# Output tiles that take the products with the high part of the activations first, and wait for them chunk by chunk

## The reference

```
h    = rmsnorm(x, norm1_g) * (1 + sc1) + sh1
q_a, k_a, v_a, beta, alpha, z_a, q_b, k_b, v_b, u_c, gates = split(h @ w_in)
o_a  = gated_deltanet(...);  o_b = differential_attention(...);  o_c = hyena(...)
merged = sum over j of sigmoid(gates_j) * (o_j @ w_br_j)
x    = x + g1 * (merged @ w_out)
hf   = rmsnorm(x, norm2_g) * (1 + sc2) + sh2
gate, up = split(hf @ w_ffn_in)
x    = x + g2 * ((silu(gate) * up) @ w_ffn_out)
```

## Time and profile before

| | us |
|---|---|
| median of 3 runs (lowest to highest) | 3982.35 (3978.43 to 3986.39) |
| the profiled execution | 3979.51 |
| its span, first to last instruction | 3977.7 |
| TensorE matmuls busy | 3424.3 (86%) |
| GpSimd busy | 1437.6 (36%) |
| VectorE busy | 1432.8 (36%) |
| ScalarE busy | 817.8 (21%) |

### The profile page before, as it was taken

The page is one execution under the profiler, slowest core; times in us unless marked ns, Lnnn a source line. Parts: engine busy times, 40 slices in busy tenths (PEclk is TensorE's granted clock), DMA queues, the critical chain, the costliest instruction groups (busy, mean ns, idle before and its releaser), DMA issues.

```text
span 3977.7 us, 55062 instructions
## 1 busy us (share of the span) xinstructions
PE 3424.3 (86%) x21792; PEld 3061.2 (77%) x21792; DVE 1432.8 (36%) x2231; ACT 817.8 (21%) x1639; POOL 1437.6 (36%) x1088
## 2 busy tenths in 40 slices
PE   6978887877889987999987888797688998799997
PEld 5967777546569987999977777684384898799996
DVE  2067773355432122111122667705553222211112
ACT  3133332232110112010022333313311111200001
POOL 0454442002215543444424444320040354344443
PEclk8989998877799998999988999997797999899999
DMA  4201112111112211222211111121120121122221
GB/s 163 75 33 43 43 43 75 56 43 51 49 39 75 75 64 53 70 76 70 77 60 58 43 43 45 52 67 44 44 77 28 53 75 64 53 75 69 70 75 69
DMA packets 62882, 242.62 MB, mean 61 GB/s; under 512 B 6961, under 2 KB 6961, under 8 KB 61489
## 3 DMA queue, kind: packets, MB, share of 16 engines
q1 hardware_dynamic: 60336, 224.77, 17.6%
q10 hardware_dynamic: 1728, 12.36, 0.8%
q0 software_dynamic: 576, 2.10, 0.2%
HBM read 234.48 MB, written 4.72 MB: 60 GB/s over the span
## 4 chain that ended last, share of the span: by engine, by line
PE 66%; issue 10%; DVE 9%; POOLq 5%; POOL 4%; ACT 2%; DVEq 2%; DMA 1%; ACTq 0%; SPq 0%
PE ps_G L582 27%; PE ps_GPM L582 26%; POOLq L2002 5%; PE ps_M L960 2%; POOL gu_hi L1985 1%; DVE small L1735 1%; PE ps_GPM L613 1%; PE ps_G L848 1%; POOL gu_lo L1985 1%; POOL big L2011 1%; PE ps_M L905 1%; PE ps_M L662 1%; DVE big L1766 1%; PE ps_M L988 1%; PE ps_M L887 1%
## 5 line engine op out<-in xcount | busy, mean ns | idle before, releaser
L1949 POOL CAST w_hi<-ring 128x1024 fp32r<-128x1024 f32 x296 | 310.1, 1048 | 1596.7 <-PE ps_G L582 983.8
L1951 POOL TENSOR_TENSOR w_lo<-ring,w_hi 128x1024 fp32r<-128x1024 f32 x296 | 740.9, 2503 | 51.8 <-issue 8.9
L582 PE MATMUL ps_G<-room_a,w_hi 128*128 128x320 f32 x1984 | 455.7, 319 | 92.6 <-DVEq L1434 61.9
L582 PE MATMUL ps_GPM<-room_a,w_hi 128*128 128x320 f32 x1984 | 437.5, 309 | 0.0
L582 PEld LDWEIGHTS ps_G<-room_a,w_hi 128*128 128x128 f32 x1984 | 346.4, 196 | 95.8 <-DVEq L1434 63.7
L582 PE MATMUL ps_G<-room_b,w_hi 128*128 128x320 f32 x1408 | 369.0, 315 | 24.0 <-DVEq L1434 24.0
L582 PE MATMUL ps_G<-room_o,w_hi 128*128 128x320 f32 x1280 | 337.4, 313 | 44.3 <-DVEq L1434 44.3
L582 PE MATMUL ps_GPM<-room_b,w_hi 128*128 128x320 f32 x1408 | 361.4, 309 | 0.0
L582 PE MATMUL ps_GPM<-room_o,w_hi 128*128 128x320 f32 x1280 | 332.9, 309 | 0.0
L582 PEld LDWEIGHTS ps_GPM<-room_a,w_hi 128*128 128x128 f32 x1984 | 331.9, 188 | 0.0
L2001 POOL TENSOR_TENSOR outs<-big,con 128x512 f32<-128x512 f32 x168 | 208.7, 1242 | 296.7 <-DVEq L1582 190.5
(11 more groups left out here) (392 smaller groups left out, 5941.4 us busy)
## 6 DMA issues: line engine op xcount, KB each, us to landing
ring<-in_W SPq DMA_DIRECT2D x416, 512.0 KB, 3.5
big<-in_INV ACTq DMA_DIRECT2D x2, 1664.0 KB, 6.8
par<-in_PARAMS ACTq DMA_DIRECT2D x2, 1646.0 KB, 8.9
big<-in_FWD ACTq DMA_DIRECT2D x2, 1632.0 KB, 8.0
x<-in_X SPq DMA_DIRECT2D x1, 2560.0 KB, 8.9
out_Y<-h SPq DMA_DIRECT2D x1, 2560.0 KB, 7.5
con<-in_CONSTS SPq DMA_DIRECT2D x1, 1364.0 KB, 11.7
sc<-in_HYCS ACTq DMA_DIRECT2D x2, 578.5 KB, 3.5
```

What stands on the lines that cost most here:

```text
L582: m = pe.matmul(ap, w[wi][:, k, n0:n0 + P], acts[ai][k][:, a:b], start=(k == 0 and i == 0), stop=(k == chunks - 1 and i == 2))
L1949: nc.gpsimd.tensor_copy(hi, raw)
L1951: nc.gpsimd.tensor_tensor(wlo[:, slot * UNIT:(slot + 1) * UNIT], raw, hi.bitcast(F32), ALU.subtract)
```

## The change

- `by_parts` goes. `tile_product` now runs in two passes over the chunks: first, for each chunk, weights-high and weights-low with the high activation; then, for each chunk, weights-high with the low activation. Inside a chunk each weight tile is used for the half in the first bank, then for the half in the second. The 48 products and their weight loads are the same.
- The first tile of a stage gets `ready`: a semaphore and a value for the high part and for the low part. Before each chunk of either pass TensorE waits for that chunk's tile. The single waits ahead of the stages go.
- `low_tiles` and the low tiles of the mix branches signal at each tile, not behind the drain; the drain stays, without a signal.
- `shift` writes each piece twice: rounded into the stage's high tiles, then shifted in place into `h`; the last of the four instructions of a chunk signals its high tile. The `round_tiles` behind norm1 (stage A) and behind norm2 (f1) go, and VectorE's wait for `h_ready` there.

```diff
-            def by_parts(ap, w, n0, acts, a, b, chunks=KC, turned=None):
-                for k in range(chunks):
-                    for i, (wi, ai) in enumerate(((0, 0), (0, 1), (1, 0))):
-                        m = pe.matmul(ap, w[wi][:, k, n0:n0 + P], acts[ai][k][:, a:b], start=(k == 0 and i == 0),
-                                      stop=(k == chunks - 1 and i == 2))
...
-                by_parts(tile[:, 0:HALF], w, n0, acts, 0, HALF, chunks, fl_a)
-                return by_parts(tile[:, HALF:NT], w, n0, acts, HALF, NT, chunks, fl_b)
+                for weights, part in (((0, 1), 0), ((0,), 1)):
+                    for k in range(chunks):
+                        if ready is not None:
+                            done, value, per = ready[part]
+                            pe.wait_ge(done, value + k // per)
+                        for wi in weights:
+                            for a, b, fl in ((0, HALF, fl_a), (HALF, NT, fl_b)):
+                                first = k == 0 and wi == 0 and part == 0
+                                m = pe.matmul(tile[:, a:b], w[wi][:, k, n0:n0 + P], acts[part][k][:, a:b], start=first,
+                                              stop=(k == chunks - 1 and part == 1))
+                                if first:
+                                    m.then_inc(fl, 1)
+                return m
...
-                pe.wait_ge(h_split.sem, h_split.at(L, 2))
                 for i in range(0, 2):
-                    products("B", "t", 0, L, i, h_b)
+                    products("B", "t", 0, L, i, h_b, ready=None if i else h_tiles(L, 1))
...
-                    pe.wait_ge(act_ready, L * (FT // 2) + ((first + n) // 2))
+                    pairs = L * (FT // 2) + first // 2 + 1
                     for i in range(0, 2):
-                        products(f"f2_{g}", "t", 0, L, i, act_f, n)
+                        products(f"f2_{g}", "t", 0, L, i, act_f, n, None if i else ((act_hi, pairs, 2), (act_ready, pairs, 2)))
...
-            def shift(layer, k0, mod_at):
+            def shift(layer, k0, mod_at, acts, sem_):
                 for k in range(KC):
                     act.wait_ge(hnorm.sem, hnorm.at(layer, k0 + k + 1))
-                    nc.scalar.activation(hv[:, k, 0:NS], hv[:, k, 0:NS], ACT.Identity,
-                                         bias=modv[:, mod_at + k, 0:1])
-                    nc.scalar.activation(hv[:, k, NS:NT], hv[:, k, NS:NT], ACT.Identity,
-                                         bias=modv[:, mod_at + k, 1:2])
+                    for q, (a, b) in enumerate(((0, NS), (NS, NT))):
+                        bias = modv[:, mod_at + k, q:q + 1]
+                        nc.scalar.activation(acts[0][k][:, a:b], hv[:, k, a:b], ACT.Identity, bias=bias)
+                        m = nc.scalar.activation(hv[:, k, a:b], hv[:, k, a:b], ACT.Identity, bias=bias)
+                    m.then_inc(sem_, 1)
                 act.drain()
...
-                shift(L, 0, 0)
+                shift(L, 0, 0, h_a, hi_ready.sem)
                 act.drain().then_inc(h_ready.sem, 1)
-                round_tiles(htiles, h_a, hi_ready.sem)
...
-                    tt(acts[1][k], src[k], acts[0][k].bitcast(F32), ALU.subtract)
-                dve.drain().then_inc(done, 1)
+                    tt(acts[1][k], src[k], acts[0][k].bitcast(F32), ALU.subtract).then_inc(done, 1)
+                dve.drain()
...
                 scale(0, L, rms_ready.at(L, 1))
-                dve.wait_ge(h_ready.sem, h_ready.at(L, 1))
                 low_tiles(htiles, h_a, hi_ready.sem, hi_ready.at(L, 1), h_split.sem)
```

More of the change, by code:

```diff
@@ L408, in trunk_program @@
         unit_split = sem("unit_split")
[L409 to L412, removed]
+        h_split = sig_("h_low_tiles_ready", 4 * KC)
+        o_split = sem("o_low_tiles_ready")
+        m_split = sig_("merged_low_tiles_ready", KC)
+        hf_split = sig_("h_ffn_low_tiles_ready", KC)
         inverse_done = sem("inverse_done")
@@ L575, in parts, with tile_product @@
                         wlo[:, lo * UNIT:(lo + 1) * UNIT].rearrange("p (k n) -> p k n", n=n))
-            def by_parts(ap, w, n0, acts, a, b, chunks=KC, turned=None):
-                for k in range(chunks):
-                    for i, (wi, ai) in enumerate(((0, 0), (0, 1), (1, 0))):
-                        m = pe.matmul(ap, w[wi][:, k, n0:n0 + P], acts[ai][k][:, a:b], start=(k == 0 and i == 0),
-                                      stop=(k == chunks - 1 and i == 2))
[L584 to L588, removed]
+            def tile_product(phase, name, t, layer, step, w, n0, acts, chunks=KC, ready=None):
                 _, fl_b = fill(phase, name + "_b", layer, step)
@@ L601, in fill, with products, h_tiles @@
                 return ap, fl
-            def products(phase, prefix, k, layer, step, acts, chunks=KC):
+            def products(phase, prefix, k, layer, step, acts, chunks=KC, ready=None):
                 for t in range(4):
                     w = parts(phase, k + t, layer, step)
-                    tile_product(phase, f"{prefix}{t}", t, layer, step, w, 0, acts, chunks).then_inc(unit_used, 1)
+                    tile_product(phase, f"{prefix}{t}", t, layer, step, w, 0, acts, chunks, None if t else ready
+                                 ).then_inc(unit_used, 1)
+            def h_tiles(layer, n):
+                return (hi_ready.sem, hi_ready.at(layer, n * KC + 1), 1), (h_split.sem, h_split.at(layer, n * KC + 1), 1)
             def modulation(k, slot, number):
@@ L664, in _ @@
                 m.then_inc(fl, 1)
-                pe.wait_ge(h_split.sem, h_split.at(L, 1))
                 for i in range(0, 4):
-                    products("A", "t", 0, L, i, h_a)
+                    products("A", "t", 0, L, i, h_a, ready=None if i else h_tiles(L, 0))
                 pe.wait_ge(g_ready.sem, g_ready.at(L, 1))
@@ L922, in _ @@
                     pe.matmul(ap[:, 0:P], ones, osq[:, NS:NT], start=True, stop=True).then_inc(fl, 1)
-                pe.wait_ge(h_split.sem, h_split.at(L, 3))
                 for i in range(0, 3):
-                    products("C", "t", 0, L, i, h_c)
+                    products("C", "t", 0, L, i, h_c, ready=None if i else h_tiles(L, 2))
                 pe.wait_ge(hyc_in.sem, hyc_in.at(L, 16))
@@ L997, in _ @@
                 m.then_inc(fl, 1)
-                pe.wait_ge(h_split.sem, h_split.at(L, 4))
                 for b in range(0, 3):
                     for half in range(2):
-                        products("mix", f"g{half}_", 6 * half, L, b, h_b)
-                        if half == 0:
-                            pe.wait_ge(o_split, L * 3 + b + 1)
+                        products("mix", f"g{half}_", 6 * half, L, b, h_b, ready=h_tiles(L, 3) if b + half == 0 else None)
+                        o_at = (L * 3 + b) * 4 + 1
                         for s in range(2):
@@ L1009, in _ @@
                             for t in range(2):
-                                m = tile_product("mix", f"b{half}_{2 * s + t}", t, L, b, w, t * P, o_m, 4)
+                                m = tile_product("mix", f"b{half}_{2 * s + t}", t, L, b, w, t * P, o_m, 4,
+                                                 ((om_hi, o_at, 1), (o_split, o_at, 1)) if half + s + t == 0 else None)
                                 if t == 0:
@@ L1013, in _ @@
                             m.then_inc(unit_used, 1)
-                pe.wait_ge(m_split.sem, m_split.at(L, 1))
                 for i in range(0, 2):
-                    products("out", "t", 0, L, i, h_b)
+                    products("out", "t", 0, L, i, h_b, ready=None if i else (
+                        (mg_hi.sem, mg_hi.at(L, 1), 1), (m_split.sem, m_split.at(L, 1), 1)))
                 sum_squares("norm2", L, hv, KC, sq_ready)
-                pe.wait_ge(hf_split.sem, hf_split.at(L, 1))
                 for g, (first, n) in enumerate(F_GROUPS):
                     for i in range(0, n // 2):
-                        products(f"f1_{g}", "t", 0, L, i, h_f)
-                    pe.wait_ge(act_ready, L * (FT // 2) + ((first + n) // 2))
+                        products(f"f1_{g}", "t", 0, L, i, h_f, ready=None if g + i else (
+                            (hf_hi.sem, hf_hi.at(L, 1), 1), (hf_split.sem, hf_split.at(L, 1), 1)))
+                    pairs = L * (FT // 2) + first // 2 + 1
                     for i in range(0, 2):
-                        products(f"f2_{g}", "t", 0, L, i, act_f, n)
+                        products(f"f2_{g}", "t", 0, L, i, act_f, n, None if i else ((act_hi, pairs, 2), (act_ready, pairs, 2)))
             sum_squares("norm1", DEPTH, hv, KC, sq_ready)
@@ L1394, in _ @@
                 rms_root("norm2", L)
-                shift(L, KC, 24)
+                shift(L, KC, 24, h_f, hf_hi.sem)
                 act.drain().then_inc(h_ready.sem, 1)
-                round_tiles(htiles, h_f, hf_hi.sem)
                 for g, (first, n) in enumerate(F_GROUPS):
@@ L1872, in _ @@
```

(4 more changed lines are left out.)

1 line of the change is left out of this document (removed).

## The result

The changed kernel takes 3892.9 us (median of 4 runs, 3892.3 to 3893.8), the kernel before beside it 3984.0 (3978.4 to 3986.4): a ratio of 0.977 [0.976, 0.979], some 91 us by the medians. The forecast was 3897, with 3882 to 3926 as range, and a sum of -85.6 us.

A forecast was written before the change was run, and what follows sets the result against it. TensorE's output-tile products, idle 130.2 and 30.6 us waiting for VectorE's queue, were taken as the bound. Terms of -42.8 us a layer, -85.6 for two, from the median 3982.35 give 3896.8 (forecast 3897); range 3882 to 3926.

The forecast's parts named there:

- A: Stage A behind norm1: the double shift writes take 1.86 us a chunk, a loss of 5.8 us per layer.
- f1: First tile of f1: ends at 1515.9 where it ended at 1520.42, -4.5 us per layer, ends -6.9 and -1.3.
- mix and out: Starts of mix and out: the first product moves earlier, -6.0 and -7.1 us per layer, each within 1.5 us.
- C: First tile of C: ends 0.4 us after the last low tile, -9.6 us per layer; low end 7.2.
- f2: Starts of the three f2 groups: waits shrink or go, -6.8, -7.6 and -6.3 us, together -20.7 us per layer.
- The clock stays low while chunks trickle in: Rival, chance 0.18: first tiles of C, mix, out and f1 run wholly at 1.2 GHz, 30 us back, 3926.
- The costly order: Rival, chance 0.06: gaps at each bank change lower the clock; with a tenth of the tiles +168 us, 4065.
- The faster pitch: Rival, chance 0.04: the new order makes all 14016 products faster, 188 us less, 3709.

The follow-up runs named there:

- the kernel with the rounds: The changed kernel with the norms of before (shift in place, then eight rounds), chunk waits kept: 3877.3 us, ratio 0.9742 against the kernel before.

## Why the prediction was right, step by step

The mechanism held: single waits for VectorE went, one for one, with the low clock behind them, and the norms' part lost in A. That the sum came within 0.4 us in the first layer is partly luck: mix and out together fell short by 2.2 us, and f1, C with the stages before it, and A made up 2.1 of it. One reading was short and entered no sum: by 0.267 us a product, first tiles of 8.67 to 10.08 us ran 3.6 to 6.8 us at the lower clock, not 3 to 6.

**f2** came out within 0.2 us in every group: 6.84, 7.62 and 6.14 us against 6.8, 7.6 and 6.3. The third group waits once for its last low pair (0.17 us, where 0.4 was worked out; then the 0.04 "issue" and the four products from 1919.18 in the chain above).

**C** was right in size and in what ends it. From ScalarE's first round the next tile starts at 11.4 us (935.95 to 947.35) where it was 20.96 (931.29 to 952.25): -9.56. The last low tile ends at 946.75 and the tile 0.6 us later. The table by stretch has the granted clock up again during the high products, so the low ones follow VectorE at full speed and the next tile does not start slow; the low end of this term's bounds was not needed:

```profile
936.80:943.00 6.20, 6.17 (x31) 6.20 (x32) 5.94 (x6) 4.28 (x7) 0.00 (x0) 0.71 0.28 75
943.00:947.30 4.30, 3.69 (x20) 2.65 (x19) 3.91 (x9) 0.00 (x0) 0.00 (x0) 1.00 0.15 62
```

Stages V and attention, whose code is as before, make the rest of that row of the table, 0.4 us in the first layer.

**mix and out** were mis-sized by 1.4 and 0.8 us, inside the 1.5 given for them. The start moved as forecast: from ScalarE's first round to the first product it is 0.88 us in place of 6.82 at mix, and 0.89 in place of 7.98 at out, -5.9 and -7.1. The term that failed is the tile itself, which I left as long as before: 9.85 in place of 8.67, and 9.67 in place of 8.91. Its surplus over 7.04, divided by the 0.12 us between 0.267 and 0.147, gives 23 and 22 products at the lower clock, where it was 14 and 16. In these rows from mix the clock stands at 0.50 (1.2 GHz) over the first 4.8 us although TensorE has almost no gap (4.74 us busy), and has risen in the stretch behind:

```profile
1146.20:1151.00 4.80, 4.74 (x18) 4.77 (x19) 4.80 (x7) 4.80 (x8) 0.00 (x0) 0.50 0.00 0
1151.00:1156.10 5.10, 5.10 (x34) 5.10 (x33) 3.91 (x3) 2.02 (x4) 0.00 (x0) 0.90 0.00 0
```

The extra products show that it is the clock. Why it takes longer than in the kernel before stays open: with the same code around it, mix's first tile took 9.86 us in one layer and 8.81 in the other of the kernel with the rounds. Over the traces without extra products it took 8.66 to 9.29 us in the eight first tiles with the single wait, and 8.55 to 9.86 us in the eight with chunk waits. The means, 9.0 and 9.5 us, lie 0.5 us apart, so much of the 1.2 us may be scatter.

**A** lost 6.1 us from the first shift to the projection's start (9.07 to 15.16) against 5.8. The chunk takes 1.81 us, not 1.86:

```profile
66.48 0.72 ACT L1096 ACTIVATE room_b<-h,modc 128x512 fp32r<-128x512 f32 x1 [5.38 <-DVEq L1493]
67.11 0.71 ACT L1097 ACTIVATE h<-h,modc 128x512 f32<-128x512 f32 x1
67.72 0.39 ACT L1096 ACTIVATE room_b<-h,modc 128x128 fp32r<-128x128 f32 x1
68.01 0.39 ACT L1097 ACTIVATE h<-h,modc 128x128 f32<-128x128 f32 x1
68.30 0.71 ACT L1096 ACTIVATE room_b<-h,modc 128x512 fp32r<-128x512 f32 x1
...
80.67 0.38 ACT L1097 ACTIVATE h<-h,modc 128x128 f32<-128x128 f32 x1
81.64 2.53 PE L667 MATMUL ps_M<-par,h 128*128 128x16 f32 x11 [21.31 <-ACTq L1106]
```

The short piece overlaps its neighbour as assumed (0.29 us apart, 0.39 long). So the chunks take 0.3 us less than forecast; between the end of the last shift and the projection lie 0.6 us, which were 0.1 before. (The table has 5.6, since this norm began 0.6 us earlier in the profiled execution.) In the second layer the loss from VectorE's first scaling to the projection is 5.6 us, but the scaling itself comes 1.3 us earlier after f2: in the kernel before, the chain goes there over the transfer of the layer's parameters (9.37 us), in the changed kernel over the sums of squares. That the second layer repeats the first was right within 0.2 us but for A and the stretch up to C. The kernel with the norms' part alone and the one without it show the loss from both sides, +9.5 and -12 us.

**f1** gained 1.5 us more than the term. The last high tile comes at 14.6 us (1479.81 to 1494.40), not 15.0. The 20 products behind it took 4.22 us, not 5.3: the clock came up while they ran, the case that I had put at the end of the bounds. In the stretches before, it had not:

```profile
1481.80:1489.00 7.20, 5.71 (x16) 4.14 (x16) 6.49 (x13) 7.20 (x17) 0.00 (x0) 0.50 0.00 0
1489.00:1494.80 5.80, 4.66 (x13) 3.46 (x14) 4.50 (x7) 5.39 (x12) 0.00 (x0) 0.50 0.00 0
1494.80:1498.70 3.90, 3.90 (x22) 3.90 (x22) 0.45 (x1) 0.00 (x0) 0.00 (x0) 0.75 0.00 0
```

What the prediction did not see is that this term has nothing to do with the direct writes: the chunk waits alone, on the old rounds, bring the same 18.8 us.

**The rivals.** "The clock stays low while chunks trickle in" holds at f1, where 29 products ran at 0.50 over 13 us, but not as a rule: in the kernel with one write in norm2 it rose to 1.00 while f1's chunks still trickled in. In C, mix and out the clock rose, and no first tile ran wholly at the low one; of its 30 us for two layers, mix and out in the first layer gave back 2 together. The costly order, and with it the time of 4065, is refuted by the kernel with the order alone: there two banks alternate at every product, with a ratio of 0.9999. The section that the prediction names with it (the Trainium skill, TensorE: Matmul & The Clock Gate, section "A second HAM failure mode: psum-queue depth-cycling") puts the swings of the clock down to small idle times in a kernel that cycles through banks. The trace agrees only so far that idle time costs the clock (f2's first tile of 8.79 us behind 5.1 us of it, in the kernel before); between the products of a steady tile, 0.1467 us apart, it shows none. The faster pitch falls by the same run.

## What to carry to other kernels

Where one engine sets the end, look in the list of waits for a single wait that covers all pieces of an input, and let the consumer wait piece by piece, in an order that uses first what comes first. (That the order is needed for it is argued here and not shown: no run had the waits without it.) A short wait costs more than it lasts: here 5.1 us of idle time cost 6 to 8 with the clock that went with it. And cost each part of a change by itself, since one that belongs to a winning change can lose, as the norms' double writes did.

## What the runs showed of the hardware

- In the changed kernel's f1, TensorE was busy 79% of 7.2 us and 80% of the next 5.8, and the clock stayed at 0.50; in the 3.9 us without a gap behind them it averaged 0.75. In the kernel with one write in norm2 the clock stood at 1.00 over 8.3 us in which TensorE was busy 68%, and at 0.50 over 2 us without a gap just after. So the busy share of a stretch does not tell its clock. In the changed kernel's projection, 17.15 us of products of 16 columns were busy throughout and left it at 0.50 too, as in the earlier trace rows.
- Extra products ahead of B, mix and out took 10 to 13 us off the time; the stretch of those at mix in the first layer shows the clock at 1.00 in the wait.
- Changing the PSUM bank at every product, with the weights used once for each bank, costs nothing measurable (0.9999 [0.9990, 1.0008]).
